# Two transformer blocks on one core: the first product of three feed-forwards, regrouped from three matmuls to two

## The reference

```
# block 1, layers 0 and 1 (F1 = 4096)
h = rms_norm(x, g_norm_mlp[l]) * (1 + sc2) + sh2
y = square(relu(h @ w_mlp_in[l])) @ w_mlp_out[l]        # 1024 -> 4096 -> 1024
x = x + gt2 * y
# block 2, layer 0 (F2 = 2816)
h = rmsnorm(x, g_ffn[0])
g, u = split(h @ w_gu_dense)                            # 1024 -> 2 x 2816
x = x + (silu(g) * u) @ w_dn_dense                      # 2816 -> 1024
```

## Time and profile before

| | us |
|---|---|
| time, median of 3 runs | 1682.89 (1682.88 to 1683.16) |
| the profiled execution: its span | 1683.2 |
| TensorE busy | 1645.1 (98%) |
| VectorE busy | 1209.9 (72%) |
| ScalarE busy | 964.2 (57%) |
| granted TensorE clock, mean | 0.997 |
| chain that ended last: share of PE | 83% |

### The profile page before, as it was taken

How to read it: one execution, slowest core, us unless ns; L and a number is a source line. 1 busy time by engine, 2 the same in 40 slices (tenths; PEclk the granted TensorE clock), 3 DMA queues, 4 the chain that set the end, 5 groups by cost and what they waited for, 6 DMA issues and landing times.

```text
span 1683.2 us, 26622 instructions
## 1 busy us (share of the span) xinstructions
PE 1645.1 (98%) x10360; PEld 1415.0 (84%) x10360; DVE 1209.9 (72%) x1530; ACT 964.2 (57%) x1275; POOL 88.4 (5%) x105
## 2 busy tenths in 40 slices
PE   8999999999999999999999999999999999999998
PEld 5767889988678999899999999899978787887876
DVE  2776877777768555658585555558588888989887
ACT  3765444355754444547564434547657777677774
POOL 2050000002400000000000000000000000000000
PEclk9999999999999999999999999999999999999999
DMA  9754788845359555653356555553357999999995
GB/s 342 262 209 166 270 283 283 282 134 200 126 201 312 187 180 195 195 177 112 115 177 207 185 183 185 188 175 116 123 175 254 341 344 332 339 323 342 345 330 173
DMA packets 266362, 381.63 MB, mean 227 GB/s; under 512 B 8299, under 2 KB 201121, under 8 KB 266258
## 3 DMA queue, kind: packets, MB, share of 16 engines
q1 hardware_dynamic: 264592, 377.26, 67.4%
q0 software_dynamic: 1104, 1.76, 0.3%
q10 hardware_dynamic: 562, 1.18, 0.2%
HBM read 379.12 MB, written 1.05 MB: 226 GB/s over the span
## 4 chain that ended last, share of the span: by engine, by line
PE 83%; DVE 8%; ACT 4%; POOL 2%; issue 2%; DMA 1%; ACTq 0%; DVEq 0%
PE bank L2213 72%; DVE w_low L1279 4%; ACT w_high L673 3%; PE bank L2272 3%; PE bank L2529 1%; PE bank L2776 1%; PE bank L2559 1%; DVE mod_sums L1397 1%; DVE turned L1360 1%; PE bank L2320 1%; DMA x<-in_x_dram 1%; POOL dilated_bias L636 1%; POOL dilated_bias L637 1%; PE bank L2327 1%; PE bank L2584 0%
## 5 line engine op out<-in xcount | busy, mean ns | idle before, releaser
L1279 DVE TENSOR_TENSOR w_low<-raw,w_high 128x2048 fp32r<-128x2048 f32 (+2 forms) x315 | 689.5, 2192 | 220.5 <-ACT w_high L673 218.6
L673 ACT ACTIVATE w_high<-raw 128x2048 fp32r<-128x2048 f32 (+3 forms) x333 | 596.5, 1797 | 213.2 <-PE bank L2213 205.5
L2213 PE MATMUL bank<-h_high,w_high 128*128 128x256 f32 x1200 | 342.0, 285 | 0.2
L2213 PE MATMUL bank<-h_low,w_high 128*128 128x256 f32 x1200 | 339.4, 283 | 0.0
L2213 PE MATMUL bank<-h_high,w_low 128*128 128x256 f32 x1200 | 339.4, 283 | 0.0
L2213 PE MATMUL bank<-w_high,h_high 128*128 128x512 f32 (+2 forms) x768 | 301.0, 392 | 9.1 <-DVE w_low L1279 8.1
L2213 PE MATMUL bank<-w_high,h_low 128*128 128x512 f32 (+2 forms) x768 | 291.8, 380 | 0.0
L2213 PE MATMUL bank<-w_low,h_high 128*128 128x512 f32 (+2 forms) x768 | 291.6, 380 | 0.0
L2213 PEld LDWEIGHTS bank<-h_high,w_high 128*128 128x128 f32 x1200 | 229.9, 192 | 4.0 <-issue 2.2
L2213 PEld LDWEIGHTS bank<-h_low,w_high 128*128 128x128 f32 x1200 | 230.0, 192 | 1.2
L2213 PEld LDWEIGHTS bank<-h_high,w_low 128*128 128x128 f32 x1200 | 229.9, 192 | 0.0
(11 more groups left out here) (358 smaller groups left out, 1809.0 us busy)
## 6 DMA issues: line engine op xcount, KB each, us to landing
raw<-in_w_gu_exp_dram SPq DMA_DIRECT2D x160, 512.0 KB, 5.5
raw<-in_w_in_dram SPq DMA_DIRECT2D x52, 1024.0 KB, 5.2
raw<-in_w_mod_dram SPq DMA_DIRECT2D x48, 1024.0 KB, 6.2
raw<-in_w_dn_exp_dram SPq DMA_DIRECT2D x40, 1024.0 KB, 6.7
raw<-in_w_mlp_in_dram SPq DMA_DIRECT2D x32, 1024.0 KB, 6.0
raw<-in_w_mlp_out_dram SPq DMA_DIRECT2D x32, 1024.0 KB, 5.0
raw<-in_w_gu_dense_dram SPq DMA_DIRECT2D x22, 1024.0 KB, 5.1
raw<-in_w_out_dram SPq DMA_DIRECT2D x16, 1024.0 KB, 5.1
```

The costliest lines, as they stand in the source:

```text
L673: return nc.scalar.activation(dst, src, ACT.Copy, scale=scale)
L1279: V.tensor_tensor(wlo[w % SPLIT][:, 0:n], raw[raw_of(w) % RAW][:, 0:n], whi[w % SPLIT][:, 0:n].bitcast(F32), ALU.subtract).then_inc(raw_us ...
L2213: ins = T.matmul(out, lhsT, rhs, start=start and i == 0, stop=stop and i == len(pairs) - 1)
```

## The change

`h_high` and `h_low` become two halves of one tensor, so that the 256 tokens of both, for one chunk k, can be the 512 columns of one matmul. For every tile f and chunk k, high weights times (high h, low h) is now one matmul of 512 columns over a whole bank, and low weights times high h one of 256 columns into the bank's second half. A tile takes a whole bank. When it is complete, ScalarE copies the second half to SBUF and VectorE adds the first half to it. Relu moves into VectorE's squaring.

```
+        def turned_halves(w, banks, waits, it=None, per=RAW, normed=None):
+            wh, wl = piece(w, it, per)
+            def block(f, k, first, last):
+                c = slice(k * S + P * f, k * S + P * f + P)
+                T.matmul(banks[f][:, :], wh[:, c], h_parts[:, :, k, :], start=first, stop=False, skip_group_check=True)
+                return T.matmul(banks[f][:, S:2 * S], wl[:, c], hhi[:, k, :], start=False, stop=last, skip_group_check=True)
+            if normed is not None:
+                for k in range(KD):
+                    if normed in LATE and k in (0, 2):
+                        turn_quarter(normed, 2 + k // 2)
+                    pe.wait_ge(h_low, KD * normed + k + 1)
+                    for f in range(2):
+                        ins = block(f, k, k == 0, k == KD - 1)
+                        if k == KD - 1:
+                            ins.then_inc(used if f else f_tile, 1)
+                return
+            for f in range(2):
+                if waits is not None:
+                    pe.wait_ge(*waits(f))
+                for k in range(KD):
+                    ins = block(f, k, k == 0, k == KD - 1)
+                ins.then_inc(used if f else f_tile, 1)
```

TensorE, block 1 (banks 0 and 1 for every block b) and dense (gate: banks 0 and 1, up: banks 2 and 3; `dense_bank` gives bank 6 for the gate's second tile of block 0):

```
-                if b >= 3:
-                    pe.wait_ge(f_one[l], loop(b - 2, it, 3))
-                turned_product(m, S, KD, [(psum[slot], 0), (psum[slot], S)], it=it, normed=None if b else 2 * l + 1)
+                turned_halves(m, psum[0:2], (lambda f: (f_sum, loop(tile_sums[l] + 2 * b - 1 + f, it, 6))) if b else None, it,
+                              normed=None if b else 2 * l + 1)
...
+            def gate_or_up(g, w, b, it=None, normed=None):
+                turned_halves(w, [dense_bank(g, f, b) for f in range(2)], (lambda f: (f_sum, loop(tile_sums[2] + 4 * b - 3 + 2 * g + f, it, 8))) if b else None,
+                              it, normed=normed)
```

ScalarE (block 1; in the dense one `copy_gate_or_up` does the same, for the gate behind `store_rs`):

```
-                nc.scalar.activation(relu[:, 0, slot, :], psum[slot][:, :], ACT.Relu).then_inc(f_one[l], 1)
+                for f in range(2):
+                    if f == 0:
+                        act.wait_ge(f_tile, loop(first_tiles[l] + b + 1, it, 3))
+                    else:
+                        act.wait_ge(used, loop(w + 2 * b, it, RAW) if b else w + 1)
+                    copy(relu[:, 0, slot, S * f:S * f + S], psum[f][:, S:2 * S]).then_inc(f_half, 1)
```

VectorE (block 1; the order of the calls around it stays):

```
+            def sum_tile(b, f, slot, it=None):
+                dve.wait_ge(f_half, loop(tile_sums[l] + 2 * b + f + 1, it, 6))
+                v = relu[:, 0, slot, S * f:S * f + S]
+                V.tensor_tensor(v, psum[f][:, 0:S], v, ALU.add).then_inc(f_sum, 1)
             def squares_of(b, slot, it=None):
-                dve.wait_ge(f_one[l], loop(b + 1, it, 3))
+                for f in range(2):
+                    sum_tile(b, f, slot, it)
+                dve.wait_ge(f_sum, loop(tile_sums[l] + 2 * b + 2, it, 6))
                 if b >= 3:
                     dve.wait_ge(f_hi[l], loop(b - 2, it, 3))
-                V.tensor_tensor(relu[:, 1, slot, :], relu[:, 0, slot, :], relu[:, 0, slot, :], ALU.mult) \
+                V.scalar_tensor_tensor(relu[:, 1, slot, :], relu[:, 0, slot, :], 0.0, relu[:, 0, slot, :], ALU.max, ALU.mult) \
                     .then_inc(f_two[l], 1)
```

More of the change, by code:

```diff
@@ L183, in program @@
     x = sb("x", [P, TT, D])
-    hhi = sb("h_high", [P, KD, S], F32R)
-    hlo = sb("h_low", [P, KD, S], F32R)
+    h_parts = sb("h_high_and_low", [P, 2, KD, S], F32R)
+    hhi, hlo = (h_parts[:, i, :, :] for i in range(2))
     heads_area = ExitStack()
@@ L349, in program, with dense_bank @@
     y_high, y_low, scattered, x_added = sem("y_high"), sem("y_low"), sem("y_scattered"), sem("x_added")
-    f_one = [sem(f"ff{i}_function") for i in range(4)]
+    f_one = {i: sem(f"ff{i}_function") for i in (2, 3)}
+    f_tile, f_half, f_sum = sem("ff_first_tile_multiplied"), sem("ff_tile_second_half_copied"), sem("ff_tile_summed")
+    first_tiles, tile_sums = (0, 16, 32), (0, 32, 64)
+    def dense_bank(g, f, b):
+        return psum[6 if (g, f, b) == (0, 1, 0) else 2 * g + f]
     f_two = [sem(f"ff{i}_product") for i in range(4)]
@@ L1104, in _, with copy_gate_or_up @@
                 norm_squares(n + 1)
+            def copy_gate_or_up(g, w, b, it=None):
+                if b >= 2:
+                    act.wait_ge((f_lo if g else f_two)[2], loop(b - 1, it, 2))
+                for f in range(2):
+                    if f == 0:
+                        act.wait_ge(f_tile, loop(first_tiles[2] + 2 * b + g + 1, it, 4))
+                    else:
+                        act.wait_ge(used, loop(w + 1, it, RAW))
+                    copy(silu[:, g, b % 2, S * f:S * f + S], dense_bank(g, f, b)[:, S:2 * S]).then_inc(f_half, 1)
             def rooted_silu(b, it=None, per=0):
@@ L1957, in _, with gate_roots, sum_tile2, product_of_sums @@
                 refine_rows(rs_done, whole=True)
[L1958 to L1965, removed]
+            def gate_roots(b, it=None, per=0):
+                v = silu[:, 0, b % 2, :]
+                for f in range(2):
+                    sum_tile2(v, f, 0, b, it, per)
+                dve.wait_ge(f_sum, loop(tile_sums[2] + 4 * b + 2, it, 2 * per))
+                v = v.rearrange("p (a s) -> p a s", s=S)
+                V.tensor_tensor(v, v, late_row.unsqueeze(1).to_broadcast([P, 2, S]), ALU.mult).then_inc(gate_out, 1)
+            def sum_tile2(v, f, g, b, it, per):
+                dve.wait_ge(f_half, loop(tile_sums[2] + 4 * b + 2 * g + f + 1, it, 2 * per))
+                v = v[:, S * f:S * f + S]
+                V.tensor_tensor(v, dense_bank(g, f, b)[:, 0:S], v, ALU.add).then_inc(f_sum, 1)
+            def product_of_sums(b, it=None, per=0):
+                v = silu[:, 1, b % 2, :]
+                for f in range(2):
+                    sum_tile2(v, f, 1, b, it, per)
+                dve.wait_ge(f_sum, loop(tile_sums[2] + 4 * b + 4, it, 2 * per))
+                dve.wait_ge(f_one[2], loop(b + 1, it, per // 2))
+                V.tensor_tensor(v, v, silu[:, 0, b % 2, :], ALU.mult).then_inc(f_two[2], 1)
             def product(f, w, b, n, it=None, per=0, wper=0, e=None):
@@ L1986, in _ @@
                 dve.wait_ge(rs_out, n + 2)
-                gate_roots(w + 1, 0)
-                product(2, w + 2, 0, 512)
+                gate_roots(0)
+                product_of_sums(0)
                 low_block2(2, 0, 512)
@@ L1992, in _ @@
                     rest_to(m + 2)
-                    gate_roots(m + 1, j + 1)
+                    gate_roots(j + 1)
                     rest_to(m + 3)
-                    product(2, m + 2, j + 1, 512)
+                    product_of_sums(j + 1)
                     rest_to(m + 4)
@@ L2001, in _ @@
                         rest(m + 2, it)
-                        gate_roots(m + 1, j + 1, it, 2, RAW)
+                        gate_roots(j + 1, it, 4)
                         rest(m + 3, it)
-                        product(2, m + 2, j + 1, 512, it, 2, RAW)
+                        product_of_sums(j + 1, it, 4)
                         rest(m + 4, it)
@@ L2690, in _ @@
             pe.wait_ge(mod_stored, stored_of(l, 5))
-            pe.wait_ge(f_one[l], last)
+            pe.wait_ge(f_sum, tile_sums[l] + 2 * last + 2)
             spread_gate(l, 1)
```

53 lines of the change are left out of this document (26 added, 27 removed).

## The result

The changed kernel takes 1685.92 us (median of 20 runs, 1684.44 to 1689.12), the kernel before 1683.11 (20 runs on the same chip, 1681.82 to 1686.32): a ratio of 1.0015, 95% interval 1.0009 to 1.0021, or 2.5 us more (1.5 to 3.5; the two medians are 2.8 us apart). The forecast was 1681.2, range 1678.3 to 1686.0. The time is inside the range, but it moved the other way: 1.7 us less was forecast. The profiled execution has a span of 1684.7 us and a mean granted clock of 0.996.

What follows compares the result with a forecast made beforehand. TensorE was taken to set the time in all three feed-forwards. Layer 0 (-0.9 + 1.7), layer 1 (0.3 + 0.35) and dense (-3.1) sum to -1.65 us on the median 1682.9: 1681.2 us, range 1678.3 to 1686.0.

Steps and rivals of the forecast that it cites:

- the saving per pair: Per tile and chunk, three matmuls of 0.120 us (0.360) become 0.227 + 0.120 = 0.347: 0.0133 us saved.
- Off TensorE: Added copies, sums and squaring, 0.9 us of VectorE per block of block 1, cost nothing in the steady state under TensorE.
- The opening waits: Feed-forward starts: TensorE waits for the new sum, about 2.8 us at up(1) in both layers, about 1.4 at gate(1).
- What is late next: Through VectorE's longer chain, down(1) starts 1.85 us late in both layers and down(2) of layer 1 2.8 us late.
- The clock: Granted clock falls after both up(1) pauses: layer 0 pays 1.7 us whole, in layer 1 0.35 remains.
- Dense: Dense feed-forward: gate(1) starts 1.1 us later, less 10 blocks x 0.427 = 4.27, so -3.1 us.
- Saves nothing: Rival: merged matmul saves nothing (operand in two runs, 0.240): about 1690.8 us, or 1689 with 2.5 ns saved; chance 0.07.
- VectorE becomes the bound: Rival, layer 0: VectorE's work rises from 148.7 to 163 of 184 us; +14.5, about 1696 us; chance 0.03.
- Dearer pauses: Rival: the dense 1.4 us pause drops the clock too, or a drop lasts twice: 1683 to 1685 us; chance 0.15.
- Clock holds: Rival: the same waits at up(1) and gate(1), but at full clock: 1679.2 us; chance 0.20.

Runs made afterwards that it cites:

- run 1: Changed kernel with high and low h of one chunk side by side, 512 columns in one run: 1685.99 us, ratio 1.0018 to the kernel before.
- run 2: Changed kernel with each tile's eight matmuls of 512 columns first, then its eight of 256: 1681.63 us, ratio 0.9992 to the kernel before.
- run 11: Changed kernel, merged only from block 3 and dense block 1 on, long and short matmuls in turn: 1677.33 us, ratio 0.9964 to the kernel before.
- Run 9: Changed kernel with a tile's matmuls ordered two of 512 columns, then two of 256, and so on: 1680.44 us, ratio 0.9983 to the kernel before.
- run 5: Changed kernel without the merge: copies, sums and banks stay, three matmuls of 256 columns again: 1690.81 us, ratio 1.0055 to the kernel before.
- run 4: Changed kernel with block 1's tiles rotating over three banks and dense gate block 0 in banks 7 and 6: 1681.97 us, ratio 0.9996 to the kernel before.
- run 3: Changed kernel plus 12 unread matmuls of 512 columns behind up(0) in both feed-forwards of block 1: 1683.94 us, ratio 0.9996 to the kernel before.
- run 6: Changed kernel with VectorE's sums and squares of block 0 ahead of the low part of w+2: 1679.49 us, ratio 0.9983 to the kernel before.
- run 8: Changed kernel with eight long matmuls before eight short and up tiles rotating over three banks: 1678.00 us, ratio 0.9972 to the kernel before.
- run 10: Changed kernel with block 0's sums ahead of the low part of w+2 and eight long matmuls before eight short: 1676.17 us, ratio 0.9960 to the kernel before.

## Why the prediction was wrong

**The step that failed: the saving per pair.** I took 0.227 for the long matmul and left 0.120 for the short one, from streams in which all matmuls are alike. In turn, the two take 0.3525 (555.47 to 561.11 for 16). I had named this price's upper bound (0.240 for the long one) but tied it to the operand's two runs, which run 1 cleared. The 720 pairs behind the starts (13 and 12 blocks of 16, 10 of 32) saved 0.0075 in place of 0.0133 each, 4.2 us less; run 2 got 4.3 back by order alone, run 11 lost 3.5 by it. That is nearly the whole distance between the forecast of -1.7 us and the +2.5 measured. Why one and one is dearer and two and two is not stays open. Run 9 rules out a fixed price for each change of length, and run 5 a price of alternating weights or of writing the same half bank twice in a row, as long as all matmuls have one length (0.120 each); no run changes the length alone.

**Off TensorE: right that it is hidden, a little too dear.** The page has VectorE at 1250.8 us, 40.9 more; it costs nothing in the steady state, since no later block waits for a sum. Its work in layer 0's window (174 to 361) is 158.6 us and not 163: the new squaring takes 0.69 us, as the old one did, not 0.75, and two additions on end 0.75 and not 0.84.

**The opening waits: right in place and size.** 3.0, 3.0 and 1.4 us for 2.8, 2.8 and 1.4. Against the kernel before up(1) of layer 0 is 2.9 us late (9.35 us after up(0), before 6.44). From the end of the first sum (181.63 and 0.42) to the start at 182.19 it takes 0.14 us, where I had left 0.06; the other 0.1 of the wait was there before, too.

**What is late next: right, but covered.** Run 4 shows VectorE's bound at down(1), +1.6 us for my 1.85; runs 3 and 6 show that of layer 1 at down(2), 0.38 and 0.64 us of waiting for my 1.4. In run 3 down(2) starts 2.4 us late by VectorE for my 2.8, and TensorE, which saved less than I had given it, comes later than I said. In the changed kernel neither wait exists, because TensorE is the later one. In layer 1 the fallen clock made it so. In layer 0 it is so at full clock as well: in run 3 down(1) starts 26.22 us after up(0) without a wait, 2.15 later than before, where I had both engines arrive at 1.85. In the changed kernel it starts 27.64 us after up(0), 3.57 later, for my 1.85 + 1.7.

**The clock: right that it falls, its size off in layer 1.** I put 1.7 us behind each pause, and 0.35 of the second. By the granted clock a drop is worth 1.7 us in these profiles (layer 0 here; both layers in run 2; 1260 in the earlier trace rows) and sometimes twice that, as in layer 1 here. What TensorE loses by it is read from the length of up(1): 1.4 to 1.6 us for a single drop, 2.6 for the double one. So layer 0 paid 1.4 for my 1.7. Layer 1 moved by +2.89 for my +0.65: down(2) starts 2.0 us later than in run 3 at full clock, where I had 0.35, 0.4 less came from VectorE (2.4 for 2.8), and 12 x 0.093 = 1.1 is the pair. Run 1, with a single drop, has down(2) 0.9 us later than run 3, so 0.35 was too little even then; part of it was a slip, since by the earlier trace rows TensorE would have waited 2.8 - 1.85 + 0.2 = 1.2 us for VectorE and not 1.4. Over the ten pauses of 3.0 us in the profiles of the changed kernel and of runs 1, 2, 5 and 9, nine drops came behind eight of them, and up(1) was 13.1 us longer in all: 1.3 us a pause. Run 3, with the same delay and full clock, is 2.0 us faster in the median, so my sum of 2.05 for both layers was about right as a mean. The Trainium skill's rule that I had named there ("TensorE: Matmul & The Clock Gate", section "HAM oscillation") agrees with eight of these ten pauses. Its figure for an isolated matmul's fixed cost (section "Back-to-back issue gap") does not fit here: by it the merge would save 2.5 ns a pair, and the runs show 7.5 in turn and 12.5 in groups.

**Dense: +1.5 at gate(1) for +1.1, and 0.22 a block for 0.427.** 10 x 0.207 = 2.1 us of the 2.7 that the stage fell short is the pair again, 0.4 the opening. The rest comes with the order in turn as well: a dense down product takes 5.50 us here, in run 4 and in run 11, and 5.47 in the kernel before and in run 2.

**The rivals.** "Saves nothing" came about by half, and for another reason than the one I gave it. "VectorE becomes the bound" did not occur. "Dearer pauses" did in layer 1 of the profiled execution; its other form, a drop behind the dense pause of 1.4 us, is in none of the eight profiles that have this pause. "Clock holds" is what run 3 comes closest to.

## What to carry to other kernels

A stream's price per matmul holds only for a stream of that make-up: where a change mixes two lengths one by one, bound the price from above and try them in groups of at least two, which here was the whole difference between loss and no change. Merging results into whole banks trades banks for matmuls, and the bill comes where no other product lies between two uses of a bank: keep the old form there and merge from the first block that has cover (8.9 us faster than before, instead of 2.8 slower). A pause of TensorE is to be priced with the clock behind it: here 1.3 us on average on top of 3.0.

## What was not expected of the hardware

- A matmul of 512 columns and one of 256 in turn, each with its own weight load, take 0.3525 us a pair; in groups of two or eight, 0.3475. The starts are then 0.24 and 0.11 to 0.12 instead of 0.2275 and 0.120.
- A moving operand in two runs of 256 columns 8 KB apart costs the same as one of 512 in a row (5.64 us an up product both ways).
- Which pause drops the clock varies from execution to execution: a pause of 3.0 us brought no drop in two cases of ten, one in seven and two on end in one; a pause of 2.2 to 2.3 us (runs 4 and 8) one in two of four; one of 1.4 us (dense) none in eight; one of 1.1 us (runs 6 and 10) none in four. A drop made up(1) 1.4 to 1.6 us longer.
- Between 1250 and 1270, in a part of the kernel that the change does not touch, six of the thirteen profiles have a drop (1.7 us by the granted clock), two of them twice that. That such drops spread the times of one kernel over 4 to 6 us is likely, but only the profiled executions show their clock.
